# A recurrent mixer's triangular inverse and scan: first blocks made per head pair, value turns moved into the solve and the scan, first norm inside the scan, finer waits at the projection

## The reference

```python
def step(S, inp):
    r_t, w_t, k_t, v_t, a_t, b_t = inp
    sa = jnp.einsum('bhij,bhj->bhi', S, a_t)
    S = S * w_t[:, :, None, :] + sa[..., None] * b_t[:, :, None, :] + v_t[..., None] * k_t[:, :, None, :]
    y = jnp.einsum('bhij,bhj->bhi', S, r_t)
    return S, y
...
mu = jnp.mean(y, axis=-1, keepdims=True)
var = jnp.mean(jnp.square(y - mu), axis=-1, keepdims=True)
y = (y - mu) * lax.rsqrt(var + GN_EPS) * gn_g + gn_b
y = y + jnp.sum(r_h * k_h * r_k, axis=-1, keepdims=True) * v_h
rwkv_out = y.reshape(B, T, RWKV_WIDTH) * g
...
mix = jnp.concatenate([pool_out, rwkv_out], axis=-1)
x = x + mix @ w_out
```

## Time and profile before

| | us |
|---|---|
| median of 3 runs | 2541.25 (2539.93 to 2542.51) |
| the profiled execution's own time | 2540.49 |
| its span (first to last instruction) | 2538.7 |
| TensorE busy / its weight loads | 2480.4 (98%) / 2252.1 |
| VectorE, ScalarE, GpSimd busy | 1331.0, 938.0, 191.1 |
| mean granted TensorE clock | 0.991 |

### The profile page before, as it was taken

How to read it: one execution, slowest core, us unless ns; L and a number is a source line. 1 busy time by engine, 2 the same in 40 slices (tenths; PEclk the granted TensorE clock), 3 DMA queues, 4 the chain that set the end, 5 groups by cost and what they waited for, 6 DMA issues and landing times.

```text
span 2538.7 us, 39896 instructions
## 1 busy us (share of the span) xinstructions
PE 2480.4 (98%) x18487; PEld 2252.1 (89%) x18487; DVE 1331.0 (52%) x1117; ACT 938.0 (37%) x862; POOL 191.1 (8%) x133
## 2 busy tenths in 40 slices
PE   7999988999999999999999999999999999999999
PEld 6998976898898998998779999777998999899897
DVE  3574536544444444445457658575554454544553
ACT  4421024433333333334444364255433433333332
POOL 0003020021020020020000001100000000000000
PEclk9999998999999999999999999989999999999999
DMA  7531014555655655656555644233564664664643
GB/s 241 185 133 68 30 68 177 192 179 186 198 177 189 198 176 190 193 190 214 182 165 173 199 156 137 81 133 133 169 196 166 202 196 149 219 196 152 217 162 133
DMA packets 317476, 425.40 MB, mean 168 GB/s; under 512 B 3914, under 2 KB 224366, under 8 KB 316670
## 3 DMA queue, kind: packets, MB, share of 16 engines
q1 hardware_dynamic: 315885, 416.59, 49.9%
q0 software_dynamic: 1136, 4.17, 0.5%
q10 hardware_dynamic: 288, 2.10, 0.2%
HBM read 420.74 MB, written 2.10 MB: 167 GB/s over the span
## 4 chain that ended last, share of the span: by engine, by line
PE 92%; DVE 4%; issue 2%; ACT 1%; SPq 0%; POOLq 0%; DMA 0%; POOL 0%; DVEq 0%; ACTq 0%
PE PS L561 78%; PE PS L549 3%; PE PS L755 2%; PE PS L733 2%; PE PS L597 1%; PE PS L678 1%; PE PS L914 1%; DVE ring_r L2047 0%; PE PS L1098 0%; PE PS L1194 0%; PE PS L626 0%; ACT arena_r L1268 0%; PE PS L1022 0%; ACT arena L1268 0%; SPq L475 0%
## 5 line engine op out<-in xcount | busy, mean ns | idle before, releaser
L561 PE MATMUL PS<-arena_r,arena_r 128*128 128x256 f32 (+1 forms) x7232 | 1639.1, 303 | 15.6 <-DVE actT_r L1969 11.8
L561 PEld LDWEIGHTS PS<-arena_r,arena_r 128*128 128x128 f32 x7232 | 1182.3, 188 | 81.1 <-DVE actT_r L1969 12.0
L1775 DVE TENSOR_TENSOR ring_r<-ring,arena_r 128x2048 fp32r<-128x2048 f32 x316 | 730.8, 2316 | 697.7 <-ACT arena_r L1268 697.7
L1268 ACT ACTIVATE arena_r<-ring 128x2048 fp32r<-128x2048 f32 (+1 forms) x396 | 694.4, 1759 | 1033.3 <-PE PS L561 1033.1
L561 PE MATMUL PS<-arena_r,ring_r 128*128 128x256 f32 x3328 | 932.4, 280 | 0.0
L561 PEld LDWEIGHTS PS<-arena_r,ring_r 128*128 128x128 f32 x3328 | 626.2, 188 | 0.0
L561 PE MATMUL PS<-ring_r,arena_r 128*128 128x512 f32 (+1 forms) x1312 | 510.4, 389 | 0.0
L561 PE MATMUL PS<-arena_r,actT_r 128*128 128x512 f32 (+1 forms) x1184 | 458.7, 387 | 0.0
L561 PEld LDWEIGHTS PS<-ring_r,arena_r 128*128 128x128 f32 x1312 | 247.7, 189 | 53.1 <-issue 1.0
L561 PEld LDWEIGHTS PS<-arena_r,actT_r 128*128 128x128 f32 x1184 | 223.9, 189 | 46.5
L561 PE MATMUL PS<-actT_r,arena_r 128*128 128x256 f32 (+1 forms) x656 | 185.1, 282 | 0.0
(11 more groups left out here) (322 smaller groups left out, 1390.9 us busy)
## 6 DMA issues: line engine op xcount, KB each, us to landing
ring<-in_w_in SPq DMA_DIRECT2D x38, 2048.0 KB, 8.0
ring<-in_w_ffn_up SPq DMA_DIRECT2D x32, 2048.0 KB, 9.5
ring<-in_w_ffn_down SPq DMA_DIRECT2D x32, 2048.0 KB, 7.9
ring<-in_w_gate SPq DMA_DIRECT2D x22, 2048.0 KB, 8.1
ring<-in_w_up SPq DMA_DIRECT2D x22, 2048.0 KB, 8.1
ring<-in_w_out SPq DMA_DIRECT2D x16, 2048.0 KB, 8.1
ring<-in_w_down SPq DMA_DIRECT2D x12, 2048.0 KB, 8.0
ring<-in_w_down SPq DMA_DIRECT2D x20, 1024.0 KB, 5.1
```

The costliest lines, as they stand in the source:

```text
L561: mm = pe.matmul(dst, r32(w, early), r32(x, early), start=first and q == 0, stop=last and q == 2)
L1268: return act.activation(dst, src, ACT.Copy, scale=scale)
L1775: v.tensor_tensor(r32(u), u, high_of(HIW[j]), ALU.subtract).then_inc(S["w_low"], counts(units, j))
```

## The change

- The first inverse blocks are made for one pair right after its two masks, by two products over 64 partitions and one addition over 128, each of 256 elements; `dt_ready` now counts four groups of two pairs, and TensorE waits for one group and for the bank that it writes.
- The value turn is a function of a chunk. Chunks 0 and 1 are turned inside the last level of the solve, between its two halves; chunks 2 and 3 at the end of the scan's chunks 0 and 1. ScalarE places two chunks before the scan, the others in it. The copy of `AR` to `G` goes from VectorE to ScalarE, ahead of the placing, and `pool_in(4)` comes after.
- In the scan, the chunk's own part of chunk 1 comes ahead of the state's part of chunk 2, and that of chunk 2 at the end of chunk 2's step.
- The second place of the state moves from `Ytok` to an unused part of the ring's slot 1.
- The norm of the first tile: sums and squares in chunk 2 of the scan between two copies of VectorE, its variance at that step's end, its root on ScalarE in the same step, its scaling after the scan. For the second tile, the first `low` of the output weights comes between the variance and the scaling.
- The first column group of the output projection no longer waits for three quarters; it waits for each quarter alone.

```diff
-    SD = [area(SD_AT, HM, C), area(16 * ZW + RW, HM, C)]
+    SD = [area(SD_AT, HM, C), ring[:, 1, 4096:4096 + HM * C].rearrange("p (m i) -> p m i", m=HM)]
...
-        pe.wait_ge(S["dt_ready"], 1)
...
         for g in range(4):
+            pe.wait_ge(S["dt_ready"], g + 1)
+            pe.wait_ge(S["score_masked"], 2 * HM - 3 + g)
             inverse_group(g, g, lambda h, m, c, e: DTi[h, m, c, :], lambda h, m, c, e: eye64[h]).then_inc(S["d_turned"], 1)
+        def turn_v(c):
+
+            for m in range(HM):
+                for e in range(2):
+                    mm = pe.matmul(PS[HALF[1 - e], 4 + c, m * C:(m + 1) * C], zv[HALF[e], m, c * C:(c + 1) * C],
+                                   eye64[HALF[e]], start=True, stop=True)
+            mm.then_inc(S["v_turned"], 1)
...
+            if last:
+                pe.wait_ge(S["v_ready"], 1)
+                for c in range(2):
+                    turn_v(c)
...
         pe.wait_ge(S["dt_added"], 4 * len(LEVELS))
-        pe.wait_ge(S["v_ready"], 1)
-        pe.wait_ge(S["z_copied"], 13)
...
-        pe.wait_ge(S["v_placed"], NCH)
-
+        pe.wait_ge(S["v_placed"], 2)
...
+            if c == 2:
+                pe.wait_ge(S["v_placed"], c + 1)
...
             mm.then_inc(S["zc_ready"], 1)
+            if 0 < c < NCH - 1:
+                chunk_part(c - 1)
+            if c == 2:
+                pe.wait_ge(S["v_placed"], NCH)
             state_part(c)
-            if c:
-                chunk_part(c - 1)
...
                 pool_half(7 + 2 * c)
+                if c < 2:
+                    if c == 0:
+                        pe.wait_ge(S["z_copied"], 13)
+                    turn_v(c + 2)
+                else:
+                    chunk_part(c)
...
         for c in range(4):
-            pe.wait_ge(S["sum_step"], SUM["out"] + c - 1)
+            if c:
+                pe.wait_ge(S["sum_step"], SUM["out"] + c - 1)
...
-        for q in range(2, 5):
-            pool_in(q)
-        for c in range(NCH):
+        def place_v(c):
             act.wait_ge(S["v_turned"], c + 1)
...
+        for q in range(2, 4):
+            pool_in(q)
+        act.wait_ge(S["f_ready"], 4 * len(LEVELS))
+        for e in range(2):
+            copy(G[HALF[e], :, e, :, 0:C], AR[HALF[e], :, :, 0:C]).then_inc(S["at_placed"], 1)
+        place_v(0)
+        place_v(1)
+        pool_in(4)
...
+            if c < 2:
+                place_v(c + 2)
+            elif c == 2:
+                group_root(0)
...
-        v.wait_ge(S["score_masked"], 2 * HM)
-        for e in range(2):
-            h = HALF[e]
-            l1 = con("level1")[h].unsqueeze(1).unsqueeze(1).broadcast_to([C, HM, NCH, C])
-            ins = v.tensor_tensor(DTi[h], G[h, :, e, :, 0:C], l1, ALU.mult)
-        link(ins)
-        dtf = DTi.rearrange("p m c j -> p (m c) j")
-        v.tensor_tensor(dtf, dtf, over(eye64, HM * NCH), ALU.add).then_inc(S["dt_ready"], 1)
-        v.wait_ge(S["dt_ready"], 1)
+            if e:
+                v.wait_ge(S["score_masked"], g + 1)
+                for k in range(2):
+                    h = HALF[k]
+                    ins = v.tensor_tensor(DTi[h, m], G[h, m, k, :, 0:C], over(con("level1")[h], NCH), ALU.mult)
+                link(ins)
+                ins = v.tensor_tensor(DTi[:, m], DTi[:, m], over(eye64, NCH), ALU.add)
+                if m % 2:
+                    ins.then_inc(S["dt_ready"], 1)
+
+        v.wait_ge(S["dt_ready"], 4)
...
         for c in range(NCH):
...
+            if c == 2:
+                group_squares(0)
...
+            if c == 2:
+                group_variance()
+
+        group_scaled(0)
+        group_squares(1)
+        group_variance()
+        low(N_OUT, (0,))
+        group_scaled(1)
...
-        low(N_OUT, (0,))
         mixer_low(0)
         low(N_OUT, (1, 2))
         mixer_low(1)
```

More of the change, by code:

```diff
@@ L782, in _ @@
         pe.wait_ge(S["dt_added"], 4 * len(LEVELS))
-        pe.wait_ge(S["v_ready"], 1)
-        pe.wait_ge(S["z_copied"], 13)
-        for c in range(NCH):
-            for m in range(HM):
-                for e in range(2):
-                    mm = pe.matmul(PS[HALF[1 - e], 4 + c, m * C:(m + 1) * C], zv[HALF[e], m, c * C:(c + 1) * C],
-                                   eye64[HALF[e]], start=True, stop=True)
-            mm.then_inc(S["v_turned"], 1)
-        pe.wait_ge(S["v_placed"], NCH)
+        pe.wait_ge(S["v_placed"], 2)
         pe.wait_ge(S["at_placed"], 2)
@@ L1445, in gate_out @@
                 .then_inc(S["gate_copied"], 1)
-        group_root(0)
+        for c in range(NCH):
+            act.wait_ge(S["u_ready"], c + 1)
+            copy(UV(c)[LO, :, 0, :], PS[LO, 1, :].rearrange("p (m i) -> p m i", m=HM)).then_inc(S["u_placed0"], 1)
+            if c < 3:
+                pool_in(5 + c)
+            if c < NCH - 1:
+                act.wait_ge(S["sd_ready"], c + 1)
+                copy(UV(c + 1)[LO, :, 0, :], SD[(c + 1) % 2][LO]).then_inc(S["s_placed0"], 1)
+            if c < 2:
+                place_v(c + 2)
+            elif c == 2:
+                group_root(0)
+            if c % 2:
+                t = c // 2
+                act.wait_ge(S["y_ready"], c + 1)
+                copy(Ytok[:, t, :].rearrange("p (m e i) -> p e m i", m=HM, e=2),
+                     PS[:, 4 + 2 * t:6 + 2 * t, :].rearrange("p e (m i) -> p e m i", m=HM)).then_inc(S["y_copied"], 1)
         high(N_OUT, (0,), free=True)
@@ L1935, in _, with group_squares, group_variance, group_scaled @@
             v.memset(UV(0)[HALF[e], :, e, :], 0.0).then_inc(S[f"s_placed{e}"], 1)
-        for e in range(2):
-            h = HALF[e]
-            v.tensor_copy(G[h, :, e, :, 0:C], AR[h, :, :, 0:C]).then_inc(S["at_placed"], 1)
+        gsq = area(8 * ZW, 16, C)
+        def group_squares(t):
+            v.wait_ge(S["y_copied"], t + 1)
+            y = Ytok[:, t, :].rearrange("p (h i) -> p h i", h=16)
+            link(v.tensor_reduce(gnm, y, AX, ALU.add))
+            link(v.tensor_scalar(gnm, gnm, 1.0 / C, None, ALU.mult))
+            link(v.tensor_tensor(y, y, along(gnm, C), ALU.subtract))
+            link(v.tensor_tensor(gsq, y, y, ALU.mult))
+        def group_variance():
+            link(v.tensor_reduce(gnv, gsq, AX, ALU.add))
+            v.tensor_scalar(gnv, gnv, 1.0 / C, GN_EPS, ALU.mult, ALU.add).then_inc(S["gn_var"], 1)
+        def group_scaled(t):
+            y = Ytok[:, t, :].rearrange("p (h i) -> p h i", h=16)
+            v.wait_ge(S["gn_root"], t + 1)
+            link(v.reciprocal(gns, gns))
+            v.tensor_tensor(y, y, along(gns, C), ALU.mult).then_inc(S["yn_ready"], 1)
         for c in range(NCH):
```

## The result

The changed kernel took 2516.34 us in the median of four runs (2513.19 to 2519.28), the kernel before 2541.53 (now with a fourth run); the ratio is 0.9901 (95% interval 0.9884 to 0.9918). Forecast were 2515.5 and a range of 2509 to 2523. The profiled execution took 2517.19 us, its span is 2515.3: 23.4 us less than before.

A forecast was written before the change was run, and what follows sets the result against it. TensorE, busy 98% of the span, was taken as the bound. Savings of 5.4 + 4.7 + 1.0 + 0.4 + 11.8 + 2.4 = 25.7 us off 2540.5 gave 2514.8, median 2515.5; 8-in-10 range 2509 to 2523.

The forecast's parts named there:

- First inverse blocks: Between first scores and first level: blocks made between masks at 2.6 us a pair would save 5.4 us.
- the prediction's own sign: What would show it wrong: VectorE's operations of 256 elements in the first inverse blocks standing at well over 0.41 us.
- the distance: From the first score matmul (L717) to the first level in TensorE's timeline: 31.4 us worked out for the changed kernel.
- Rival 2: First inverse blocks: small operations cost 0.8 us each, 3.9 a pair; 5.4 gained become 3 lost, 2524 us; chance 6%.
- Value turn: Between solve and scan: half the turn goes into the solve, the rest into the scan; 4.7 us saved.
- Scan: In the scan's chunks: turns fill the 0.99 us stops and chunk 3 loses its own part; 1.0 us saved.
- Norm, mixing, projection: After the scan: 0.4 us of gate stop, 11.8 of wait before the output projection and 2.4 of clock saved.
- Rival 1: Output projection: a wait before the third quarter replaces the old one, TensorE stops 2.0 us, 2517.5 us; chance 8%.
- rival 3: Where transposes meet the output projection: the clock falls anyway, 2518 us; chance 8%.
- rival 4: Solve and turns: small matmuls outrun TensorE's instruction supply, 2.4 us stops in 16 groups, slower at 2553 us; chance 2%.
- rival 5: Second column group: saved time given back as a stop of about 25 us where w_out's second unit lands; chance 2%.
- the -1.5 of the rest: The span after the projection's first 120 matmuls, where a change of 0 was forecast.

## Why the prediction was right, step by step, and where it was not

- **First inverse blocks: wrong.** The step that failed is the bound on the cost of a pair. I took 2.6 us from an operation of the same size and 3.0 as the worst that GpSimd beside it could do. The first pair cost 5.66 (212.28 to 217.94), and the step's gain of 5.4 became a loss of 0.8. By the prediction's own sign (an operation of 256 elements well over 0.41) it was wrong here. The reason I missed stood in the prediction: I let the shared interface push GpSimd back and not VectorE, and I took a slowing by some 15% of a pair (3.0 against 2.6) where it is a full stop until the other's instruction has ended. GpSimd's and VectorE's rows of the kernel before, which a reader could have asked for, show both:

```profile
212.31 4.18 POOL L2470 TENSOR_TENSOR arena<-arena 128x2048 f32<-128x2048 f32 x1 [69.15 <-DVE arena L1837]
...
231.30 2.50 POOL L2480 TENSOR_TENSOR xs<-xs 128x256 f32<-128x256 f32 x1 [4.98 <-ACT xs L1268]
233.88 2.15 POOL L2482 TENSOR_TENSOR xs<-xs,cst 128x16 f32<-128x16 f32 x1
...
228.74 4.59 DVE L1908 TENSOR_TENSOR arena<-arena,cst 64x2048 f32<-64x2048 f32 x2
```

  An instruction of 4.18 us starts where the new products were to start. And beside VectorE's long operations (the products until 233.33, the addition of the earlier trace rows until 235.94) GpSimd's two small ones took 2.50 and 2.15 us, each ending within 0.5 us behind VectorE's, where 0.61 and 0.22 are their times alone. So the trace of the kernel before already had the full stop, the other way round. The rest of the working held: the later pairs took 2.55 to 3.0, and with the hold out of the scores' way the distance is 31.3 where I had 31.4. Rival 2 had the right place (the small operations beside GpSimd) and the wrong shape, eight equal delays instead of one long one.
- **Value turn: right,** 5.2 in the profile (6.2 less the 1.0 by which a stop put down to issue got shorter) for 4.7. What I missed is that the 2.2 us stop can bring the clock down as well; an execution in which it does gains 1.5 more.
- **Scan: right in kind,** 1.8 for 1.0. The turns filled the stops of 0.99 us and the squares of the norm fitted their gap: VectorE's next state update began at 357.18, 0.1 behind their end. Most of the further 0.8 comes from the order: with the chunk's part ahead of the state's, the stretch from the start of `zc` to the end of `u` takes 5.0 instead of 5.3 us in chunk 1 (332.90 to 337.92 against 337.94 to 343.25 in the chain) and as much less in chunk 2. In the chain the matmuls of neighbouring lines there alternate, so the groups overlap; that this is the reason was not tried.
- **Norm, mixing, projection: right.** TensorE goes from the last transpose to the projection without a stop. The third quarter's input was done at 395.2, wanted at 396.2. Rival 1 did not come: `mixer_low` of the second quarter began 1.0 after the projection's start (0.6 in the working). The start ran at the full clock, 27.62 us for 120 matmuls, so rival 3 fell too. The windows from 384.9 to 388 show it:

```profile
384.90:388.00 3.10, 3.10 (x17) 2.53 (x16) 1.84 (x4) 1.16 (x2) 0.34 (x1) 1.00 0.80 317
```

- **Instruction supply (rival 4) and the loads (rival 5)** cost nothing. The prediction's "one such stop" was a misreading: the view of the earlier trace rows has one of 4.2 us at L1180 too, and the chain one of 1.5 us at 1582 us. No term of the sum used them. The one in the solve was 1.4 instead of 2.4; the one at 1582 us is missing after the change. That is about the -1.5 of the rest, and it is chance: in a second profile of the same changed kernel it is back (1.4 us).
- **The total was closer than its terms, and that is luck.** The median is 0.8 from the forecast, but by the profiled executions the gain is 23.3, not 25.7, and the changed kernel's second set of runs has a median of 2518.5. A miss of 6.2 us in one term was covered in part by 1.6 us that the other mechanisms gave beyond their sums and 2.5 us of issue stops, and the median's last 2 us by four runs that fell low.

## What to carry to other kernels

Before a VectorE operation with two SBUF inputs is moved to another time, look at what GpSimd runs at that time: here what was left of its long two-input multiply was the price of the first product that met it. Put work that others wait for ahead of what may be held: here the same hold then cost TensorE 0.7 us instead of 4.3. And read each wait of an engine that is the bound for what it really needs: here one wait for three quarters, ahead of a wait for each, was half of the gain.

## What the hardware showed

- A GpSimd multiply of 128x2048 with two SBUF inputs (4.17 us) held a VectorE product of two SBUF inputs until it ended (3.33 and 3.39 us for 0.42), at two different places; VectorE's masks, with one input from PSUM, ran beside it at 0.62 to 0.65 us each, as without it. The other way round, GpSimd's operation of 128x16 took 2.15 us instead of 0.22 beside a VectorE addition of 128x2048. Beside GpSimd's one-input operations of 128x256 (0.99 us each) a pair of products took 0.85 to 1.03 us, where 0.85 is the undisturbed figure: no hold until their end is seen there.
- A stop of TensorE of 2.2 us was followed by a granted clock of 0.63 and 0.64 over the next 3 to 5 us in two profiles and by 1.00 in a third. Behind the same stop of 4.3 us the half pooling tile of 3.72 took 5.79, 5.83, 5.90, 4.32 and 4.50 us in five profiles. So the price of a stop is not its length alone, and it differs from run to run.
